# First block's attention with both heads of a pair side by side; state space outputs inside the last turn; another order of weight loads

## Time and profile before

| | |
|---|---|
| median of the runs | 2742.26 us |
| profiled execution, its own time | 2741.92 us |
| its span, first to last instruction | 2740.1 us |
| TensorE busy | 2625.4 us (96%) |
| TensorE's weight loads | 2049.0 us (75%) |
| VectorE, ScalarE, GpSimd busy | 1267.8, 934.5, 975.3 us (46, 34, 36%) |
| mean granted TensorE clock | 0.979 |
| transfers | 249.05 MB, mean 91 GB/s |

### The profile page before, as it was taken

How to read it: one execution, slowest core, us unless ns; L and a number is a source line. 1 busy time by engine, 2 the same in 40 slices (tenths; PEclk the granted TensorE clock), 3 DMA queues, 4 the chain that set the end, 5 groups by cost and what they waited for, 6 DMA issues and landing times.

```text
span 2740.1 us, 34043 instructions
## 1 busy us (share of the span) xinstructions
PE 2625.4 (96%) x11390; PEld 2049.0 (75%) x11390; DVE 1267.8 (46%) x2016; ACT 934.5 (34%) x1306; POOL 975.3 (36%) x382
## 2 busy tenths in 40 slices
PE   5999898999999999999999999999999998999997
PEld 3677566787788887776688888788887776688886
DVE  8644335435431345658732235531345658631333
ACT  3343324423422234443432223422234443422231
POOL 1232232444344443122244444244443222244442
PEclk9999999999999999999999999999999999999998
DMA  5221451232123232111123322133231112123232
GB/s 215 75 69 61 173 203 61 92 115 92 62 98 116 92 103 73 39 54 62 62 92 105 102 93 99 62 98 109 95 104 54 54 46 77 62 93 101 96 105 73
DMA packets 66981, 249.05 MB, mean 91 GB/s; under 512 B 8401, under 2 KB 10449, under 8 KB 65649
## 3 DMA queue, kind: packets, MB, share of 16 engines
q1 hardware_dynamic: 66928, 248.39, 26.9%
HBM read 244.89 MB, written 2.10 MB: 90 GB/s over the span
## 4 chain that ended last, share of the span: by engine, by line
issue 69%; POOL 15%; PE 14%; POOLq 1%; DVE 0%; ACT 0%; DVEq 0%
POOL w_lo L407 15%; PE unit_bank L444 4%; PE unit_bank L442 4%; PE unit_bank L443 4%; PE score L525 1%; POOLq L411 1%; DVE x L1627 0%; DVE unit_bank L1625 0%; POOLq L406 0%; PE mix L491 0%; PE stat_bank L499 0%; PE out_bank L491 0%; ACT arena L834 0%; PE mix L499 0%; DVE f L1608 0%
## 5 line engine op out<-in xcount | busy, mean ns | idle before, releaser
L407 POOL TENSOR_TENSOR w_lo<-raw,w_hi 128x1024 fp32r<-128x1024 f32 (+2 forms) x378 | 975.1, 2580 | 1737.7 <-ACT w_hi L817 1737.7
L442 PE MATMUL unit_bank<-u_hi,w_hi 128*128 128x512 f32 x2160 | 854.9, 396 | 16.7 <-POOL w_lo L407 8.4
L443 PE MATMUL unit_bank<-u_lo,w_hi 128*128 128x512 f32 x2160 | 843.9, 391 | 0.0
L444 PE MATMUL unit_bank<-u_hi,w_lo 128*128 128x512 f32 x2160 | 843.8, 391 | 0.0
L817 ACT ACTIVATE w_hi<-raw 128x1024 fp32r<-128x1024 f32 (+2 forms) x378 | 418.2, 1107 | 1128.2 <-PE unit_bank L444 1094.0
L442 PEld LDWEIGHTS unit_bank<-u_hi,w_hi 128*128 128x128 f32 x2160 | 407.5, 189 | 123.6 <-issue 32.2
L444 PEld LDWEIGHTS unit_bank<-u_hi,w_lo 128*128 128x128 f32 x2160 | 407.5, 189 | 86.0
L443 PEld LDWEIGHTS unit_bank<-u_lo,w_hi 128*128 128x128 f32 x2160 | 407.5, 189 | 85.9 <-issue 2.9
L442 PE MATMUL unit_bank<-h_hi,w_hi 128*128 128x512 f32 x992 | 390.0, 393 | 16.6 <-POOL w_lo L407 11.3
L443 PE MATMUL unit_bank<-h_lo,w_hi 128*128 128x512 f32 x992 | 386.9, 390 | 0.0
L444 PE MATMUL unit_bank<-h_hi,w_lo 128*128 128x512 f32 x992 | 386.8, 390 | 0.0
(11 more groups left out here) (295 smaller groups left out, 2150.6 us busy)
## 6 DMA issues: line engine op xcount, KB each, us to landing
raw<-in_w_gate_up SPq DMA_DIRECT2D x168, 512.0 KB, 3.3
raw<-in_w_down SPq DMA_DIRECT2D x64, 704.0 KB, 4.1
raw<-in_w_in SPq DMA_DIRECT2D x66, 512.0 KB, 3.3
raw<-in_w_up SPq DMA_DIRECT2D x32, 512.0 KB, 3.3
raw<-in_w_out SPq DMA_DIRECT2D x24, 512.0 KB, 3.4
f<-in_w_ada_rows SPq DMA_DIRECT2D x22, 512.0 KB, 4.5
raw<-in_w_down SPq DMA_DIRECT2D x16, 512.0 KB, 3.3
ada_late<-in_w_ada_rows SPq DMA_DIRECT2D x10, 512.0 KB, 5.0
```

The costliest lines, as they stand in the source:

```text
L407: e.tensor_tensor(w_lo[:, s, 0:n], raw[:, s, 0:n], as32(w_hi[:, s, 0:n]), ALU.subtract).then_inc(lo_ready, 1)
L442: e.matmul(bank[:], wh, hi(k), start=n == 0, stop=False)
L443: e.matmul(bank[:], wh, lo(k), start=False, stop=False)
L444: mm = e.matmul(bank[:], wl, hi(k), start=False, stop=last)
```

## The change

- In the turns both heads' blocks of equal width go together: block n belongs to query block n // 2 and head n % 2, so the widths are 128, 128, 256, 256, and so on. Score banks, the two bias tables and the `pT` areas exist once for each head. `values` is one call a turn, whose matmuls alternate between the heads, behind the first unit of the next turn. The turns are written out, without `Fori`.
- State space outputs: `outputs(0)` and `outputs(1)` stand behind the second and third unit in the last turn, in `stat_bank`; ScalarE's gelu comes ahead of the next refill. The inputs stand behind the next unit, the K products behind the first two units in turn 0; VectorE grows C after the tables of the scan.
- The start: the masks of `tabs` are loaded after the third `w_ada` chunk, the rest after all; the first weight tiles after the sixth. Squares are added in pairs and the four sums go through TensorE. The reciprocal (`invert(0)`) stands ahead of growing B; the first refills ahead of taking the modulation's row.
- Weight loads: pair 2 goes between the 16 transfers of `us`; pairs 3 and 4 ahead of the wait for K. The modulation's other loads and parts: none ahead of the merge, one behind each of its units, two behind the first unit of `w_out`, one behind each of the next six; `w_merge`'s first load ahead of them.

```diff
@@ SyncE
+                if k == 2:
+                    e.dma_start(tabs[:, 0:MASKS], d["tabs"][:, 0:MASKS]).then_inc(masks_loaded, 16)
+                if k == 5:
+                    for s in range(2):
+                        load(0, s, d["w_in"][s], D)
+            e.dma_start(tabs[:, MASKS:], d["tabs"][:, MASKS:]).then_inc(consts_loaded, 16)
...
-            load_pairs(2, d["w_in"], 4, 1)
+                if m == 1:
+                    load_pairs(2, d["w_in"], 4, 1)
+            load_pairs(3, d["w_in"], 6, 2)
             e.wait_ge(k_taken, 2)
...
-            load_pairs(3, d["w_in"], 6, MERGE1 - 3)
+            load_pairs(5, d["w_in"], 10, MERGE1 - 5)
             e.wait_ge(y_taken, 2)
...
-            for n in range(3):
-                load_ada(n)
             for u in range(2 * DC):
                 load(p + u % DC // 2, u % 2, w[u % DC], w.shape[2])
-                if 1 <= u < 2 * DC - 2:
-                    load_ada(u + 2)
+                if u == 0:
+                    load_ada(0)
+                if u < 2 * DC - 1:
+                    load_ada(u + 1)
@@ TensorE
+                if k in (2, 3):
+                    e.wait_ge(masks_loaded, 16)
+                    for c in (2 * k - 4, 2 * k - 3):
+                        e.wait_ge(x_added, c + 1)
+                        mm = e.matmul(stat_bank[:], tab("ones"), x_sq[:, 2 * c, :], start=c == 0, stop=c == 3)
...
+            def values(j):
+                e.wait_ge(v_ready, j + 1)
+                e.wait_ge(pT_ready, 8 * j + 8)
+                for b in range(TB):
+                    for i in range(b + 1):
+                        for h in range(2):
+                            rows = slice(HD * h, HD * h + HD)
+                            mm = e.matmul(out_bank[rows, b * P:(b + 1) * P], v_nat[:, i, rows], pT(h, b)[:, i, :],
+                                          start=i == 0, stop=i == b)
+                mm.then_inc(pv_done, 1)
+            for j in range(HEAD_PAIRS):
                 in_unit(in_pair(j, 0), 1)
+                if j:
+                    values(j - 1)
+                else:
+                    inputs()
                 in_unit(in_pair(j, 1), 0)
+                if j == 0:
+                    e.wait_ge(bu_ready, 4)
+                for h in range(2):
+                    scores(j, h)
                 turn_v(o_taken, j + 1, taken[0], in_pair(j, 1) + 2, v_turned)
                 for n, (p, s) in enumerate(((1, 1), (2, 0), (2, 1), (3, 0))):
                     in_unit(in_pair(j, p), s)
+                    if j == 0 and n < 2:
+                        within_stride(n)
+                    if j == HEAD_PAIRS - 1 and n in (1, 2):
+                        outputs(n - 1)
+                    for h in range(2):
+                        turn_probs(j, 2 * n + h)
+                    if n < 3:
+                        for h in range(2):
+                            scores(j, 2 * n + 2 + h)
...
             in_unit(in_pair(HEAD_PAIRS, 0), 1)
+            values(HEAD_PAIRS - 1)
             in_unit(in_pair(HEAD_PAIRS, 1), 0)
+            e.wait_ge(consts_loaded, CONSTS)
             e.wait_ge(gelu_ready, 2)
@@ ScalarE, from the turns on
+            for j in range(HEAD_PAIRS):
+                heads(j)
             for m in range(2):
                 e.wait_ge(y_ready, m + 1)
                 e.activation(gelu_y[:, m, :], ssm_y[:, m, :], ACT.Gelu_apprx_tanh).then_inc(gelu_ready, 1)
+            refill(in_pair(HEAD_PAIRS, 1), 1)
+            take_out(HEAD_PAIRS - 1)
+            gate(1, 3 * HEAD_PAIRS + 1)
@@ VectorE
+            for c in range(0, DC, 2):
+                e.wait_ge(x_squared, c + 2)
+                e.tensor_tensor(x_sq[:, c, :], x_sq[:, c, :], x_sq[:, c + 1, :], ALU.add).then_inc(x_added, 1)
...
+            invert(0)
             grow(B_grown, STRIDE, b_bar[:, 0, :, :], b_bar[:, 1, :, :], False)
...
             step(e.memset(decays[:, :, 0:1], 0.0))
+            grow(C_grown, STRIDE + 1, per_state("c_re"), per_state("c_im"), True)
+            e.sem_inc(C_ready, 1)
+            settled()
             e.wait_ge(bu_ready, 4)
```

More of the change, by code:

```diff
@@ new lines, in outputs @@
+            def outputs(n):
+                e.wait_ge(scan_ready, 2 * n + 2)
+                e.wait_ge(within_loaded, 16 * STRIDE)
+                if n:
+                    e.wait_ge(y_taken, 1)
+                for m in range(4):
+                    i, at = 4 * n + m, m * P
+                    e.matmul(stat_bank[:, at:at + P], within[:, i, :], us_chunk[:, i, :], start=True, stop=False)
+                    for part in range(2):
+                        mm = e.matmul(stat_bank[:, at + 1:at + P],
+                                      C_grown[:, part, i, 1:STRIDE + 1, :].rearrange("p m c -> p (m c)"),
+                                      states[:, part, i, 0:CHUNKS - 1], start=False, stop=part == 1)
+                mm.then_inc(y_done, 1)
@@ new lines, in scores @@
+            def scores(j, n):
+                b, h = divmod(n, 2)
+                if n == 0:
+                    for s in range(2):
+                        e.wait_ge(taken[s], in_pair(j, 0) + 2)
+                if n >= 2:
+                    e.wait_ge(s_biased, 8 * j + n - 1)
+                rows = slice(HD * h, HD * h + HD)
+                e.matmul(score[h][:, 0:(b + 1) * P], q_st[rows, b * P:(b + 1) * P],
+                         k_st[rows, 0:(b + 1) * P], start=True, stop=True).then_inc(s_done, 1)
@@ L751, in ada_rest_part @@
                 ada_part(1 + n // DC, n % DC, ada_rest[n % 3], mix[n // DC])
-            for n in range(2):
-                ada_rest_part(n)
             for c in EIGHT:
@@ L1301, in amplify @@
                                             col(g_name, 0, 8), ALU.add, ALU.mult))
-            def invert(st):
-                e.wait_ge(std_ready, st + 1)
-                step(e.reciprocal(rstd[:], std))
-            invert(0)
             take_mod(0, score[0])
@@ L1329, in _ @@
             modulate(0, 0)
-            grow(C_grown, STRIDE + 1, per_state("c_re"), per_state("c_im"), True)
-            e.sem_inc(C_ready, 1)
             def squared(re, im):
@@ L1390, in scan_parts, with split_out, heads @@
                 return turned, scanned
-            with e.Fori(0, HEAD_PAIRS) as j:
-                start = step.enter(j, HEADS1_STEPS)
-                def bias(h):
-                    step(e.tensor_scalar(bias_h, tab("dist"), col("slopes", 2 * j + h), None, ALU.mult))
+            def split_out(j):
+                e.wait_ge(ohi_ready, j + 1)
+                e.tensor_tensor(h_lo[:, j, :], out_bank[:], as32(h_hi[:, 7 + j, :]), ALU.subtract).then_inc(o_taken, 1)
+            def heads(j):
                 def score_bias(n):
-                    b = n % TB
+                    b, h = divmod(n, 2)
                     W = (b + 1) * P
@@ L1433, in _ @@
                     take_probs(n)
-                    if n + 2 == TB:
-                        bias(1)
                     if n + 2 < 2 * TB:
@@ L1444, in _ @@
                         tiles[n // 2]()
-                e.wait_ge(ohi_ready, j + 1)
-                e.tensor_tensor(flat(h_lo[:, bass.ds(j, 1), :]), out_bank[:],
-                                as32(flat(h_hi[:, bass.ds(7 + j, 1), :])), ALU.subtract).then_inc(o_taken, 1)
-            step.at = start + HEAD_PAIRS * HEADS1_STEPS
+            for j in range(HEAD_PAIRS):
+                heads(j)
             e.wait_ge(y_loaded, 16 * 4 * STRIDE)
```

208 lines of the change are left out of this document (86 added, 122 removed).

## The result

Four runs of the changed kernel took 2703.88 to 2706.43 us, median 2705.27; four of the kernel before, on the same chip, 2741.53 to 2744.22, median 2742.52. The ratio is 0.9863, with a 95% interval of 0.9846 to 0.9880: 37.3 us less, where 31.5 (to 2711) were forecast. The median lies near the low end of my own range, 2704 to 2716. The profiled execution took 2703.88 us against 2741.92 before, 38.0 us less. This is the gain that the rest of the text splits up; its span is 2702.1 us and the mean granted clock 0.979, as before. One execution of the kernel with values one head after the other took 9247 us, with a granted clock of 1.00; it is left out of that kernel's range, median and rows.

What follows compares the result with a forecast made beforehand. Turns bound by TensorE's work, their end by a ScalarE, SyncE queue and VectorE chain, the first turn's beginning by VectorE. Three turns 15.0 + first turn 2.5 + tail 13.7 = 31.2 us off 2741.9: forecast 2711, own range 2704 to 2716.

Steps and rivals of the forecast that it cites:

- Step 1: Value products in each turn: two heads on alternating column halves run at once, saving 2.35 us a turn.
- Step 2: Scores in each turn: two heads on different row halves run at once, saving 1.92 us a turn.
- Rivals A and D: Turns: A, scores' row halves don't run at once, 2718, chance 0.14; D, neither scores nor values do, 2728, 0.06.
- Step 3: Order in each turn: values behind the next unit remove a 0.90 us wait, less 0.2 charged for touching a GpSimd split.
- Step 4: First turn, bound by VectorE: 5.2 - 2.8 - 1.9 + 2.0 = 2.5 us saved, bounds -3 to +6.
- Step 5: State space outputs and merge loads: waits of 3.4 and 8.8 us go, clock gives 2.0, 0.5 charged: 13.7 us.
- Rival B: Tail: another wait replaces the 8.8 us before the merge, a third to all comes back: 2720, chance 0.12.
- Step 6: The rest (written-out turns, weight load queue, SyncE's wait for K): nothing gained or lost.
- Rival C: Turns: equal-width softmax outgrows its unit, TensorE rests and its clock falls; 2744 or 2777, chance 0.06.

## Why the prediction was right

**The bound.** A turn is bound by TensorE's own work and the gain arrives at the end: right, but for the 1.9 us given back. At the modulation's third row the changed kernel is 39.96 us ahead. From there on both kernels run the same instructions, and TensorE is idle for only 1.0 us more in the changed one; yet its lead moves both ways. In times of the kernel before it is 38.2 at 452 us, 39.8 at 1110, 40.7 at 1300 to 2150, 39.7 at 2340 and 38.0 from 2380 to the end. Where it falls most the rest ahead is equally long in both (7.03 and 7.02 us in the first case, 0.87 each in the second), and the clock isn't the same. The kernel before, from the same instruction on as the rows of after:
```profile
429.10:434.10 5.00, 4.96 (x15) 3.99 (x16) 4.89 (x8) 2.17 (x3) 0.00 (x0) 0.65 0.01 3
2352.90:2362.90 10.00, 9.98 (x33) 6.49 (x34) 8.97 (x18) 6.87 (x11) 2.35 (x1) 0.66 0.24 79
```
The kernel after:
```profile
389.10:394.10 5.00, 4.92 (x12) 3.94 (x13) 4.89 (x8) 2.17 (x3) 0.00 (x0) 0.50 0.00 0
2313.20:2323.20 10.00, 9.97 (x30) 7.19 (x31) 7.89 (x16) 5.75 (x9) 2.35 (x1) 0.51 0.23 79
```
So the same rest costs one or two microseconds more or less from kernel to kernel, and the 1.9 are what such moves, and 1.0 us of idle time, happen to add up to. They are as large in the experiments: the kernel with late additions is 3.4 us behind after at the third row, 0.2 near 1350 us, and 3.4 again at the end; the one with C grown later is 4.1 ahead at the first token sums of the feed-forward part, 7.0 near 1310 us and 6.7 at TensorE's last instruction.

**Step 1 (values).** 2.37 us for 2.35, of two parts: 1.8 from halves running at once, 0.57 from one group instead of two. The size held, the reason only for three quarters of it; the rest is luck.

**Step 2 (scores).** 1.93 for 1.92. The estimate from column quarters held for row halves. Rivals A and D fall.

**Step 3 (order).** The 0.90 us wait went and the 0.2 charged for touching a split didn't come: in the widest step the last scan part starts just ahead of the split, and in the narrower steps the chain had room. What I missed is 0.96: "the order here changes mode no oftener than before" was wrong. Each step went from probabilities, scores, probabilities, scores to two and two, six changes a turn fewer. The Trainium skill's "TensorEngine Tiling (Array Packing)", Tiling Modes, says that a change of tiling mode drains the engine; the trace agrees, with 0.16 us a change, if the change is what costs. I had this rule before me and counted the changes wrongly.

**Step 4 (first turn).** The step that missed, by 6.4 us: forecast 2.5, measured 8.9, beyond its own bound of +6. I put the additions at 20.73, where the trace of before has them, while the diff puts them at 16.70: 3.2 us, shown by moving them back. The other 3.2 are the clock, which gave 4.4 us where I had put 2.0 (2.4), the fewer changes that I hadn't counted (1.0), and the first probabilities, which my sum had at 98.4 and which came at 98.0 with late additions (0.4). That is 3.8, and the 0.7 us by which the account of the first turn is over bring it to 3.1; what these 0.7 are stays open.

**Step 5 (outputs and loads).** 3.4 + 10.3 forecast. 10.3 came at the merge. That is the right sum with the wrong working: I gave the 8.8 us to the two edits together, where the outputs' place alone took 6.4 of the 10.3, and the order of loads alone takes the whole wait from the kernel before. With the turn's own 6.1 taken off, the fourth turn gave 2.3 and not 3.4; 0.8 of the lack is the new wait ahead of the outputs. Both spares were near: 7.1 for 5 and 1.2 for 1.8. Rival B had the narrow place right, and it held.

**Step 6** stood at nothing, and no stretch shows anything of it.

**Rival C**, the only one on the other side, had its condition in the first turn alone: a rest of 5.1 us, with the clock low in the K product behind it, and never in a turn's third or fourth unit. That it decides from a rest of some 3.5 us on is not borne out: with the outputs late, a rest of 1.9 us was followed by a gate product of 5.37 us instead of 3.59.

The profiled gain was 6.8 us over the sum of 31.2: 6.4 from the first turn and 2.3 from the second and third, less 1.9 given back at the end. So the time came near by the large terms, two of which (the values and the fourth turn) have their size partly by luck, and the one part that I worked out instruction by instruction was the one that missed.

## What to carry to other kernels

Products that use half the rows or half the columns of TensorE are to stand next to their complement, and small products of one kind together: here two heads side by side gave 3.7 us of a 49 us turn, grouping another 1.5, and a wait that an order removes 0.9. Read for each moved instruction where the diff puts it, not where the old trace shows it. Where edits gain 2 to 3 us each, compare the times at which an engine reaches the same instruction and not the runs alone: a moved start changes where the clock falls after rests, and this hides or doubles such gains.

## What the hardware showed

- Row halves run at once as column halves do: 512-wide score pairs 1.13 us against 1.98 on the same rows; values 2.40 against 4.20.
- VectorE is not slowed by GpSimd's split, it is held: two operations that took 1.42 us together at 37.91 us of the kernel with late additions lasted 5.42 beside two splits (28.08 us, above). In the kernel after those splits end at 30.19 and 32.95 us and the two operations at 30.74 and 33.50, each 0.55 us later. The bias table, made from one tile in SBUF and a column, is held too: 2.17 us instead of 0.49, at 162.85 us beside a split that ends at 164.75. Operations that read TensorE's banks pass freely: 0.69 and 0.55 us at 155.68 and 155.01.
- A rest of 1.9 us was followed by 5.37 us for a gate product that takes 3.59; in another kernel a wait of 2.5 us was followed by a window at 1.00, and one of 3.8 by a window at 0.79. The length of the last rest alone does not tell the clock.
- After rests of equal length, 7.0 us in one place and 0.87 in another, the same work began at 0.65 and 0.66 of the full clock in one kernel and at 0.50 and 0.51 in the other.
